# Two of the modulation's twelve chunks are summed over k-tiles on VectorE instead of TensorE

## The reference, cut to what matters

```
mod = silu(c) @ w_ada + b_ada              # c: (1, 1024), w_ada: (1024, 6144)
sh1, sc1, g1, sh2, sc2, g2 = split(mod, 6) # 1024 each
u  = rmsnorm(h) * (1 + sc1) + sh1
z  = u @ w_in                              # retention and attention inputs
ga, gb = split(sigmoid(u @ w_gate + b_gate), 2)
h  = h + g1 * ((ga * y_ret + gb * y_dsa) @ w_o)
u2 = rmsnorm(h) * (1 + sc2) + sh2          # for the experts
h  = h + g2 * moe(u2)
```

## Time and profile before

| | us |
|---|---|
| median of 3 runs | 735.8 (735.67 to 735.87) |
| the profiled execution's own time | 736.06 |
| its span in the profile | 734.3 |
| PE busy | 711.9 (97%) |
| DVE busy | 515.1 (70%) |
| ACT busy | 380.3 (52%) |
| POOL busy | 40.5 (6%) |

### The profile page before, as it was taken

The page is one execution under the profiler, slowest core; times in us unless marked ns, Lnnn a source line. Parts: engine busy times, 40 slices in busy tenths (PEclk is TensorE's granted clock), DMA queues, the critical chain, the costliest instruction groups (busy, mean ns, idle before and its releaser), DMA issues.

```text
span 734.3 us, 9981 instructions
## 1 busy us (share of the span) xinstructions
PE 711.9 (97%) x3798; PEld 575.7 (78%) x3798; DVE 515.1 (70%) x761; ACT 380.3 (52%) x549; POOL 40.5 (6%) x52
## 2 busy tenths in 40 slices
PE   4999999999999999999999999989999999999997
PEld 2887666768888877888878777769888887888886
DVE  1456897546677774875668988987998665656854
ACT  3334435554536344564357877748534547644442
POOL 0002110010020000000000000011003400000000
PEclk9999999999999999999999999999999999999999
DMA  9999688588346931756679999945544574545541
GB/s 283 348 282 384 241 304 299 198 318 312 116 144 211 359 118 57 233 187 187 197 241 334 367 357 362 375 167 155 150 130 136 164 219 141 172 135 186 169 140 58
DMA packets 104893, 164.06 MB, mean 223 GB/s; under 512 B 10896, under 2 KB 53613, under 8 KB 104718
## 3 DMA queue, kind: packets, MB, share of 16 engines
q1 hardware_dynamic: 102942, 155.54, 63.9%
q0 software_dynamic: 1904, 7.90, 3.2%
HBM read 162.33 MB, written 1.08 MB: 223 GB/s over the span
## 4 chain that ended last, share of the span: by engine, by line
PE 82%; DVE 9%; ACT 3%; DMA 3%; issue 1%; SPq 0%; POOL 0%; ACTq 0%; DVEq 0%; POOLq 0%
PE p L559 23%; PE p L561 22%; PE p L560 22%; DVE s_rawr L1844 3%; PE p L628 2%; PE p L617 2%; PE p L1234 2%; DMA s_raw<-in_w_gate_dram 2%; PE p L698 1%; PE p L674 1%; DMA s_GS<-in_w_ada_dram 1%; PE p L1063 1%; ACT s_hi L1395 1%; ACT s_L L1445 1%; PE p L686 1%
## 5 line engine op out<-in xcount | busy, mean ns | idle before, releaser
L1844 DVE TENSOR_TENSOR s_rawr<-s_raw,s_hi 128x1024 fp32r<-128x1024 f32 x240 | 287.0, 1224 | 47.6 <-ACT s_hi L1395 46.9
L1395 ACT ACTIVATE s_hi<-s_raw 128x1024 fp32r<-128x1024 f32 x240 | 245.5, 1055 | 115.5 <-PE p L561 47.7
L559 PE MATMUL p<-s_hi,s_Ah 128*128 128x512 f32 (+1 forms) x464 | 187.3, 404 | 1.1 <-DVE s_rawr L1844 0.7
L561 PE MATMUL p<-s_hi,s_Al 128*128 128x512 f32 (+1 forms) x464 | 179.7, 387 | 0.0
L560 PE MATMUL p<-s_rawr,s_Ah 128*128 128x512 f32 (+1 forms) x464 | 179.4, 387 | 0.0
L559 PEld LDWEIGHTS p<-s_hi,s_Ah 128*128 128x128 f32 x464 | 87.2, 188 | 28.8 <-issue 8.8
L561 PEld LDWEIGHTS p<-s_hi,s_Al 128*128 128x128 f32 x464 | 87.1, 188 | 18.5
L560 PEld LDWEIGHTS p<-s_rawr,s_Ah 128*128 128x128 f32 x464 | 87.4, 188 | 15.9 <-issue 0.5
L559 PE MATMUL p<-s_hi,s_Bh 128*128 128x512 f32 x192 | 76.3, 397 | 0.5 <-DVE s_BI L2411 0.3
L561 PE MATMUL p<-s_hi,s_Bl 128*128 128x512 f32 x192 | 75.0, 391 | 0.0
L560 PE MATMUL p<-s_rawr,s_Bh 128*128 128x512 f32 x192 | 74.8, 390 | 0.0
(11 more groups left out here) (377 smaller groups left out, 850.1 us busy)
## 6 DMA issues: line engine op xcount, KB each, us to landing
s_raw<-in_w_in_dram SPq DMA_DIRECT2D x80, 512.0 KB, 4.7
s_raw<-in_w_exp_gate_dram SPq DMA_DIRECT2D x64, 256.0 KB, 4.1
s_raw<-in_w_exp_up_dram SPq DMA_DIRECT2D x64, 256.0 KB, 5.0
s_raw<-in_w_exp_down_dram SPq DMA_DIRECT2D x32, 512.0 KB, 5.7
s_GS<-in_w_ada_dram SPq DMA_DIRECT2D x12, 1024.0 KB, 7.4
s_raw<-in_w_gate_dram SPq DMA_DIRECT2D x16, 512.0 KB, 9.5
s_GS<-in_w_ada_dram SPq DMA_DIRECT2D x8, 512.0 KB, 9.2
s_raw<-in_w_ret_out_dram SPq DMA_DIRECT2D x8, 512.0 KB, 3.6
```

The costliest lines, as they stand in the source:

```text
L559: pe.matmul(o, xh, wh, start=start, stop=False)
L561: return pe.matmul(o, xl, wh, start=False, stop=stop)
L1395: act.activation(T.hi[:, i % NHL, :], T.raw[:, i % NRAW, :], ACT.Copy).then_inc(*S.hi(i))
L1844: dve.tensor_tensor(T.lo[:, i % NRAW, :], T.raw[:, i % NRAW, :], T.hi[:, i % NHL, :].bitcast(F32), ALU.subtract).then_inc(*S.lo_dve(i))
```

## The change

DVE takes over the multiplication of chunks 8 and 9. In eight steps (`ada_part`) it multiplies a k-tile of the weights (128 by 512) by its column of silu(c) and adds it to SN. What is left is one sum over the 128 partitions, which PE's transposes and DVE's `ada_end` perform: it now adds all 128 numbers of each transposed column, 512 per partition. `ada_product(8)` and `(9)` leave PE, `ada_copy(8)` and `(9)` leave ACT. `ada_used` for the halves 16 to 19 is now the fourth or the eighth of DVE's steps. PE's `ada_spread(9)` moves from behind ga0,2 to behind ga1,1. On DVE the addition `gate("ga0")` stands behind the low part of gb0,1 instead of gb0,0, and the additions to `mcols` and `mc` follow one piece later.

```diff
 def ada_used(S, j):
-    return S.ada.at("p", j if j < 8 else j | 1)
+    return S.dve_ada.at("acc", j // 2, 4 * (j % 2) + 3) if 16 <= j < 20 else S.ada.at("p", j if j < 8 else j | 1)
...
     def ada_spread(i):
-        ada_sum(i, T.SN[:, :], S.act_ada.at(i))
+        ada_sum(i, T.SN[:, :], S.dve_ada.at("acc", i, 7) if i in (8, 9) else S.act_ada.at(i))
...
     logits(1, 1)
-    uses("rg1", 2, 3, A, u)
-    ada_product(8)
-    uses("rg1", 3, 4, A, u)
+    uses("rg1", 2, 4, A, u)
     chunk_freed("rg1", S.act_gate.at("rg1", 0), S.act_gate.at("rg1", 1))
     uses("ga0", 0, 1, A, u)
     ada_spread(8)
-    uses("ga0", 1, 2, A, u)
-    ada_product(9)
-    uses("ga0", 2, 3, A, u)
-    ada_spread(9)
+    uses("ga0", 1, 3, A, u)
     att_turn("dsa", S.act_dsa, S.dve_dsa, 1, 0)
...
         uses("ga1", h, h + 1, A, u)
+        if h == 1:
+            ada_spread(9)
...
     exps(S.act_dsa, S.dve_dsa, 1)
-    ada_copy(8)
     his_to(AT["ga0", 3])
     gate_silu(S.act_gate, "rg1", lambda tt: T.RGS[:, tt, 512:1024], roped)
     his_to(AT["ga1", 1])
-    ada_copy(9)
     his_to(AT["ga1", 2])
...
+    def ada_part(n, js):
+
+        for j in js:
+            h = j // 4
+            w, c = ada_place(T, 2 * n + h)[:, j % 4, :], T.CS[:, j, 0:1]
+            q.wait_ge(*S.ada_in[h].at(2 * n + h))
+            if j:
+                q.wait_ge(*S.dve_ada.at("acc", n, j - 1))
+                dve.scalar_tensor_tensor(out=T.SN[:, :], in0=w, scalar=c, in1=T.SN[:, :], op0=ALU.mult, op1=ALU.add).then_inc(*S.dve_ada("acc", n, j))
+            else:
+                q.wait_ge(*S.ada.at("s", n - 1))
+                dve.tensor_scalar(T.SN[:, :], w, c, None, ALU.mult).then_inc(*S.dve_ada("acc", n, j))
+
     def ada_end(n):
...
-            v = T.PM[1][:, :].rearrange("p (j g c) -> p j g c", j=4, g=4)[:, :, :, 0]
+            v = T.PM[1][:, :].rearrange("p (j g) -> p j g", j=4) if n > 7 else T.PM[1][:, :].rearrange("p (j g c) -> p j g c", j=4, g=4)[:, :, :, 0]
...
     lows_to(AT["ga0", 0])
+    ada_part(8, range(0, 2))
     logits(S.dve_dsa, S.pe_dsa, 1, 0, S.dve_dsa.at("bias", 1))
     lows_to(AT["ga0", 1])
     logits(S.dve_dsa, S.pe_dsa, 1, 1, S.dve_dsa.at("bias", 1))
     maxima(S.dve_dsa, 1)
     lows_to(AT["ga0", 3])
+    ada_part(8, range(2, 8))
     recips(S.dve_dsa, S.act_dsa, 1)
+    lows_to(AT["ga1", 1])
     ada_end(8)
+    ada_part(9, range(0, 4))
     lows_to(AT["ga1", 2])
+    prob(S.dve_dsa, S.pe_dsa, "dsa", 1, 0)
+    lows_to(AT["ga1", 3])
+    ada_part(9, range(4, 6))
+    prob(S.dve_dsa, S.pe_dsa, "dsa", 1, 2)
+    lows_to(AT["gb0", 0])
+    ada_part(9, range(6, 8))
+    weighted(S.dve_dsa, S.pe_dsa, T.DO, 1)
+    lows_to(AT["gb0", 2])
     ada_end(9)
+    gate("ga0")
+    lows_to(AT["gb0", 3])
     q.wait_ge(*S.dve_ada.at(9))
...
-    lows_to(AT["ga1", 2])
-    prob(S.dve_dsa, S.pe_dsa, "dsa", 1, 0)
-    lows_to(AT["ga1", 3])
-    prob(S.dve_dsa, S.pe_dsa, "dsa", 1, 2)
-    lows_to(AT["gb0", 0])
-    weighted(S.dve_dsa, S.pe_dsa, T.DO, 1)
-    lows_to(AT["gb0", 1])
-    gate("ga0")
-    lows_to(AT["gb0", 3])
     cols("C", 0, T.Ch, T.Cl), cols("C", 2, T.Ch, T.Cl)
```

## The result

The changed kernel takes 745.36 us (745.27 to 746.99, 4 runs) against 735.84 (735.67 to 736.76, 4 runs) on the same chip: ratio 1.0132, 95% interval 1.012 to 1.0145. It is slower by 9.5 us. The profiled execution took 745.37 us, its span is 743.4. Of all executions on record one, of experiment 10, took 1433.79 us; it is in a slow state and is compared with nothing.

What follows compares the result with a forecast made beforehand. PE, busy 97% of the span, was taken as the bound. With pauses of 6.3 and 3.6 us, ga1,0 starts 6.6 us later and spread 9 costs 0.4 more: 7.0 us, so 742.8 us, range 739.8 to 746.5.

Steps and rivals of the forecast that it cites:

- The likeliest case: DVE's late steps make PE wait twice: 7.0 us slower, 742.8 us, own range 741 to 744, chance 0.58.
- the first rival: Half clock on PE behind the second pause adds 2.5 us: 745.3 us, chance 0.22.
- What leaves PE: Products 8 and 9 and a wait for ACT's copy leave PE: 1.86, 2.34 and 0.24, together 4.4 us.
- What a step costs: One DVE step takes 0.75 us busy, 0.78 start to start, bounds 0.65 and 0.8; a chunk's first 0.5 to 0.75.
- Chunk 8's steps, PE's first pause: Six steps behind DVE's low part of ga0,2 end at 161.4 us; PE idles 6.3 us before spread 8.
- SP's queue: Halves 18 and 19 wait for DVE's steps; ga0,3 behind them lands at about 167.8 us, pieces about 1.3 us apart.
- The turn (1, 2): DVE's sum and steps ahead of prob(1, 0) delay this turn to 176.5 us; PE waits 3.6 us.
- The clock: Slow PE clock behind the pauses: zero for the first; 0 to 2.5 us for the second, taken as 0.
- POOL and the biases: Bias loads wait for chunk 9's last step, land at 193.4 us; gate("ga0") stays hidden with 1.4 us to spare.
- Sum: Whole kernel shifts by 7.0 us: 743.06 us for the profiled execution, 742.8 against the median.
- The second rival: Loads overlap better and DVE's steps take 0.65 us; prob(1, 0) at 173.2, shift 3.7 + 0.4: 740.0 us, chance 0.12.
- The fourth rival: DVE's steps are hidden and PE saves its 4.4 us, needing step 7 before 155.1: 731.4 us, chance 0.03.

Runs made afterwards that it cites:

- experiment 10: Kernel of before, both products left on PE, with ACT's high part of ga0,2 ahead of the exponentials and SP's halves 18 and 19 behind ga0,3: 735.07 us.
- Experiment 9: Changed kernel, all 16 steps kept on DVE but rearranged, ACT's high part of ga0,2 ahead of the exponentials, SP's half 19 behind ga0,3 to ga1,2: 731.49 us.
- experiment 4: Changed kernel with SP's loads of halves 18 and 19 behind those of ga0,3 to ga1,2: 739.77 us.
- experiment 1: Changed kernel with 28 unused transposes of the identity on PE ahead of the turn (1, 2): 744.16 us.
- experiment 2: Changed kernel with unused transposes in both pauses, 52 ahead of spread 8 and 28 ahead of the turn (1, 2): 744.16 us.
- experiment 8: Kernel of before with chunk 9 alone summed on DVE, chunk 8 left as PE's product: 739.80 us.
- experiment 5: Changed kernel with DVE's sum for chunk 8 and all steps of chunk 9 behind prob(1, 0) and prob(1, 2): 745.41 us.
- experiment 6: Changed kernel with ACT's high part of ga0,2 ahead of the exponentials instead of behind them: 742.81 us.
- experiment 3: Changed kernel with PE's transposes of chunk 8 behind ga0,2 instead of behind ga0,0: 745.57 us.

## Why the prediction was right, point by point

The likeliest case was 742.8 us, and the range 739.8 to 746.5 held 745.36. The likeliest case's own range, 741 to 744, did not hold it. What came is nearest to the first rival, half clock behind the second pause, which had been put at 745.3 with a chance of 0.22. That its number fits to 0.1 us is luck: it has 2.5 us for the clock, which cost 1.6, and nothing for the 1.1 us that the loads added.

- **What leaves PE, 4.4 us.** Right in size. Experiment 9, where nothing took its place, is 4.6 us faster than before, but 1.0 of that may be its order (experiment 10). With that order in both, the products are worth 3.6 us by the medians and 4.6 in the two traces.
- **What a step costs.** 0.752 us for one (14 of them, 0.744 to 0.753) against 0.75, and 0.80 from start to start in the row of six (4.75 us) against 0.78. The first step, with one tensor operand, took 0.480. The Trainium skill, VectorE: DVE Perf Modes, "The perf-mode tier table (the rule you actually need)", has fp32 operations with one tensor from SBUF at twice the rate of those with two, 1.227 against 2.293 us for 2048 numbers, without a row for this operation. A quarter of that difference is 0.27 us, an estimate from the page for 512 numbers; the two durations here differ by 0.27.
- **Chunk 8's steps, PE's first pause.** Step 7 was to end at 161.4; it ended at 160.8, which is 161.5 with the 0.69 us of the earlier start. The pause was to be 6.3 us and was 6.49.
- **SP's queue.** Confirmed by experiment 4. ACT started on ga0,3 at 167.45, so 168.1, against 167.8. But ga1,0 came 2.0 us behind it, not 1.3, and DVE waited 0.77 us for it: the time between two pieces was a term of the sum that was too small.
- **The turn (1, 2).** Forecast 176.5, measured 176.92, so 177.6. The wait was 4.08 us against 3.6.
- **The clock.** This is the term that was mis-sized: taken at zero, with 2.5 as its upper bound, it was 1.6 us in the trace and 1.2 to 1.6 by experiment 1. The step that failed was "nearest to the gaps of about 1 us that left no mark": the pause of 3.6 us was weighed as though it were near 1. The row after the idle start had the size of the slowing right, about half speed, but as evidence of the clock it was weaker than the text took it: the profile of before grants 1.00 from the start to 20 us, over those slow matmuls too. That the first pause's share is off the path was right (experiment 2). The Trainium skill, TensorE: Matmul & The Clock Gate, "HAM oscillation — how this bites in real kernels", has waits between groups of matmuls put the array back to half its clock each time. The traces agree for the pauses of 6.49 and 4.08 us here, and not for the shorter waits of 1.92 us (experiment 2) and 1.40 (experiment 8), behind which the granted clock stayed at 1.00.
- **POOL and the biases.** The loads were issued at 182.93, landed 10.6 us later, and were hidden, with 3.2 us to spare: `gate("ga0")` ended at 194.8 and gb0,0 started at 198.03. That a PE which comes sooner would meet this limit follows from the 1.4 us to spare in the prediction; I forgot it in what I expected of experiment 5, where it took back nearly the whole gain.
- **Sum.** 7.0 us forecast, 9.7 measured in the stretch: 1.1 us from the loads (0.3 from ga0,3, 0.8 from ga1,0) and 1.6 from the clock.

The second rival's sum has a slip: its prob(1, 0) ends at 173.2, 3.2 us behind 169.99 and not 3.7, so it should read about 739.5, just below the range.

The fourth rival, faster at 731.4, asked for step 7 by 155.1. In experiment 9 step 7 ends at 154.1 and the time is 731.49, but that kernel also has the loads and DVE's later steps moved. That the condition alone would do is not shown, and experiment 6 speaks against it: with the steps 4 us sooner (the last ends at 156.8), the wait at the turn (1, 2) was still 4.01 us. That the two times agree to 0.1 us is partly luck, as the 4.6 us gained hold some of the new order.

Not settled: why the loads come later in the experts' stage of experiment 6, which costs it some 1.3 us far behind the change.

## What to carry to other kernels

Work that moves to an engine with idle time goes to a place in that engine's order, and the idle time in front of a wait for a late input is not available to what is put behind it. Follow each released semaphore, too: here the moved steps also held a load queue and a bias load, and three limits stood behind each other, so that removing the longest wait, or the last one, gained nothing. When PE is the bound, a pause costs its length and, where it lasted 2.3 us or more in these traces, some slow microseconds behind it unless a later wait takes them up.

## What the runs showed of the hardware that was not expected

- A pause of 2.33 us, behind the short matmuls of `ret_scores`, was enough to lower PE's granted clock (0.65 in the stretch behind it, experiment 5); pauses of 2.47 and 2.92 us did so too (experiments 6 and 8: 0.50 from 156.9 to 158.0 us, and 0.66 from 170.4 to 175.4). In the profiled execution of experiment 3 a pause of 1.82 us left it at 1.00:

```profile
177.17 1.09 PE L686 MATMUL p<-s_blob,s_L 128*128 128x128 f32 x8 [1.82 <-DVE s_PP L1943]
```

- Transposes that compute nothing kept the clock up (1.00 behind the 28 of experiment 1 and the 52 and 28 of experiment 2): with them, a kernel that does more on PE was 1.2 us faster.
- In a pause the clock was still granted in full for a while. In the changed kernel's first one it fell 2.8 us after PE had stopped, with 3.7 us still to go; its second one stood at 1.00 to the end (173.0 to 176.9 us), and the low level came 0.7 us after PE had begun again. So the clock in the pause itself does not say what it will cost behind it.
